# A two-block transformer kernel: the first expert routing in two passes, and the order of the first heads rewritten

## What is computed

```
def peer_ffn(xn, w_pq, sub_keys1, sub_keys2, expert_down, expert_up):   # per block of 128 tokens
    qh = (xb @ w_pq).reshape(T, P_HEADS, 2, P_KEY_DIM)                   # 8 heads, two half queries
    s1, s2 = qh[:, :, 0] @ sub_keys1.T, qh[:, :, 1] @ sub_keys2.T        # 128 scores each
    v1, i1 = top_k(s1, 16); v2, i2 = top_k(s2, 16)
    top_s, pos = top_k(v1[..., :, None] + v2[..., None, :], 16)          # best 16 of the 256 sums
    eidx = (i1 * 128 + i2) at pos
    g = softmax(top_s)
    a = gelu(expert_down[eidx] . xb)
    return sum_k (g * a)_k * expert_up[eidx]_k
```

## Time and profile before

| | us |
|---|---|
| median of three runs | 1513.57 |
| the profiled execution's own time | 1514.97 |
| its span | 1513.2 |
| granted clock, mean over the run | 0.912 |
| busy in the span: PE, DVE, POOL, ACT | 1266.0, 970.1, 510.4, 350.0 |
| moved by DMA | 389.60 MB, of which the gathers' queue 278.15 MB |
| first gather issued | 855.24 |
| last dot product starts | 1504.50 |

### The profile page before, as it was taken

The page is one execution under the profiler, slowest core; times in us unless marked ns, Lnnn a source line. Parts: engine busy times, 40 slices in busy tenths (PEclk is TensorE's granted clock), DMA queues, the critical chain, the costliest instruction groups (busy, mean ns, idle before and its releaser), DMA issues.

```text
span 1513.2 us, 14840 instructions
## 1 busy us (share of the span) xinstructions
PE 1266.0 (84%) x5254; PEld 907.0 (60%) x5254; DVE 970.1 (64%) x1897; ACT 350.0 (23%) x718; POOL 510.4 (34%) x407
## 2 busy tenths in 40 slices
PE   8999999999999999999999998665755666556656
PEld 6776778888888888887888896222222222222222
DVE  7799985153410000324422499999999998999987
ACT  3443433222100000123412332111111211111112
POOL 3367771010000000000010256666545555555550
PEclk9999999999999999999999999888687777887788
DMA  6232333253344444333264499999999999999997
GB/s 265 84 112 84 112 115 137 88 195 139 139 158 148 156 150 151 135 133 112 84 241 180 166 405 414 421 421 421 422 422 422 421 423 422 422 421 422 422 421 298
DMA packets 55018, 389.60 MB, mean 257 GB/s; under 512 B 6192, under 2 KB 6512, under 8 KB 8240
## 3 DMA queue, kind: packets, MB, share of 16 engines
q0 software_dynamic: 38400, 278.15, 44.4%
q1 hardware_dynamic: 16416, 110.64, 20.6%
q10 hardware_dynamic: 144, 0.03, 0.0%
HBM read 387.75 MB, written 1.05 MB: 257 GB/s over the span
## 4 chain that ended last, share of the span: by engine, by line
PE 52%; DVE 21%; DMA 18%; POOL 4%; issue 3%; ACT 2%; DVEq 0%; ACTq 0%; POOLq 0%
PE psD L992 12%; DMA arena<-in_expert,arena 9%; PE psD L935 8%; PE psD L1036 7%; PE psD L416 7%; DMA ring<-in_expert,arena 5%; DMA feat<-in_expert,arena 4%; PE psD L1009 4%; DVE arena L2090 3%; DVE feat L2090 2%; POOL arena L2079 2%; PE psD L1595 2%; DVE ring L2090 2%; PE psD L1366 2%; DVE feat L2123 2%
## 5 line engine op out<-in xcount | busy, mean ns | idle before, releaser
L992 PE MATMUL psD<-feat,ring 128*128 128x256 f32 (+1 forms) x1056 | 234.0, 382 | 5.7 <-DVE feat L370 5.2
L992 PEld LDWEIGHTS psD<-feat,ring 128*128 128x128 f32 x1056 | 201.4, 191 | 34.8 <-issue 6.5
L2079 POOL DMA_INDIRECT feat<-in_expert,arena x77 | 107.9, 1401 | 178.8 <-DVE arena L2050 156.9
L2324 POOL DMA_DIRECT2D feat<-in_xo x3 | 1.7, 554 | 443.4 <-PE psN L345 443.4
L2079 POOL DMA_INDIRECT arena<-in_expert,arena x102 | 132.2, 1296 | 38.1 <-issue 26.8
L2090 DVE CUSTOM_DVE_ANT_0 arena<-arena,feat 128x1024 f32<-128x1024 f32 x102 | 121.5, 1222 | 24.2 <-DMA arena<-in_expert,arena 23.9
L935 PE MATMUL psD<-feat,ring 128*128 128x256 f32 (+1 forms) x576 | 133.5, 390 | 0.0
L1884 PE MATMUL psB<-arena 128*128 128x512 f32 x128 | 82.8, 805 | 50.9 <-ACT arena L1977 50.9
L935 PEld LDWEIGHTS psD<-feat,ring 128*128 128x128 f32 x576 | 108.7, 191 | 24.7 <-issue 8.1
L416 PE MATMUL psD<-feat,ring 128*128 128x256 f32 x512 | 110.8, 379 | 0.0
L1036 PE MATMUL psD<-feat,ring 128*128 128x256 f32 x512 | 110.7, 379 | 0.0
(11 more groups left out here) (559 smaller groups left out, 2201.8 us busy)
## 6 DMA issues: line engine op xcount, KB each, us to landing
ring<-in_w SPq DMA_DIRECT2D x101, 1024.0 KB, 4.8
feat<-in_xo POOLq DMA_DIRECT2D x3, 1024.0 KB, 8.4
feat<-in_pq POOLq DMA_DIRECT2D x2, 1024.0 KB, 11.5
arena<-in_expert,arena POOLq DMA_INDIRECT x102, 22.5
feat<-in_expert,arena POOLq DMA_INDIRECT x77, 19.5
feat<-in_xT SPq DMA_DIRECT2D x2, 544.0 KB, 4.5
arena<-in_w_akv POOLq DMA_DIRECT2D x1, 1024.0 KB, 5.3
feat<-in_memT POOLq DMA_DIRECT2D x1, 1024.0 KB, 5.8
```

Of the source, the lines that this page charges most:

```text
L992: mm = nc.tensor.matmul(psD[:, 2 * (c % 2) + m, 0:T], home[:, k, m * P:(m + 1) * P], x[:, k], start=(k == 0), stop=(k == KT - 1))
L2079: (nc.gpsimd.indirect_dma_start(GPAIR[b], None, a["expert"], bass.IndirectOffsetOnAxis(ap=EID[:, c:c + 1], axis=0)) .then_inc(s_gb[b], 16))
```

## The change

The pieces, by the names above:

- **Routing of group 0 in two passes** (`route_first_dve`, `chosen_dve`). The best 8 keys of each half give 64 sums, whose best 8 are places 0 to 7; their indices are written first. A second pass then finds keys 9 to 16, all 256 sums, blanks the 8 sums that were taken and picks places 8 to 15. `s_eid` rises twice for group 0, so later waits read g + 2.
- **`SOON` has eight buffers in place of nine**, each used twice in group 0. The waits of the first gathers are spread: place 3 waits for `s_xt`, place 4 for `s_xo` (before, place 0 did). The load of the weights `pq5`, 1 MB, which POOL issued ahead of all gathers, stands between places 5 and 6.
- **Block 0's first score is issued in the middle of the second half query.**
- **Head 1's queries come ahead of block 1's head 0 query** on PE: chunk 0 of `pq`, `xturn`, `scores(1)`, then `query0(1, ...)`; block 1's head 0 scores are issued in the middle of the next chunk.
- **ACT's order**: the first Gelu stands before block 1's second state copy; the Gelu of group 0's quarters 2 and 3 stands before the drain of chunks 2 and 3 (it stood before the drain of chunk 3 and before the scores of head 5); Exp of group 1 and its first Gelu are each one head earlier.
- `rstd_dve(1)` on DVE moves behind quarter 1's dots.

```diff
-SOON = [4, 5, 6, 9, 10, 11, 12, 0, 3]
+SOON = [4, 5, 6, 7, 9, 10, 11, 12]
...
-    QBANK = {(0, 0): psB[:, 1], (0, 1): psD[:, 0], (1, 0): psB[:, 0], (1, 1): psB[:, 1]}
-    SBANK = {(0, 0): psD[:, 1], (0, 1): psD[:, 2], (1, 0): psD[:, 2], (1, 1): psD[:, 3]}
+    QBANK = {(0, 0): psB[:, 1], (0, 1): psD[:, 0], (1, 0): psB[:, 0], (1, 1): psD[:, 3]}
+    SBANK = {(0, 0): psD[:, 1], (0, 1): psD[:, 2], (1, 0): psB[:, 0], (1, 1): psY[:, :]}
...
@@ blocks_pe
         query0_pe(0, 0)
-        query0_pe(0, 1)
-        score0_pe(0, 0)
+        query0_pe(0, 1, mid=lambda: score0_pe(0, 0))
         score0_pe(0, 1)
...
         hturn_pe(1, 1)
-        query0_pe(1, 0)
-        query0_pe(1, 1)
-        xturn_pe(1)
-        score0_pe(1, 0)
-        score0_pe(1, 1)
...
@@ blocks_act
         first_gate()
         state_act(1, 0)
+        first_gelu()
         state_act(1, 1)
...
         state_root_act(1)
-        first_gelu()
-        for m in range(2):
-            query0_act(1, m)
-        xturn_act(1)
-        for x in range(2):
-            score0_act(1, x)
+        nc.scalar.activation(F7[:, 1, 3:4], epsc[:, 0:1], ACT.Gelu)
...
@@ peer_pe
+            if h == 1:
+                xturn_pe(1)
+                scores(1)
+                query0_pe(1, 0)
+                query0_pe(1, 1)
...
@@ peer_act
         for h in range(1, PH):
+            if h > 2:
+                scored(h - 1)
+            if h in (3, 4):
+                coefficients(0, h - 1)
+            if h == 5:
+                gate(1)
             if h == 6:
-                coefficients(0, 3)
-            if h > 1:
-                scored(h - 1)
-            if h == 4:
-                coefficients(0, 2)
-            if h == 6:
-                gate(1)
-            if h == 7:
                 gelu(1, 0)
             pair_act(FIRST["pq"], h - 1, QH[:, 2 * h:2 * h + 2])
             if h == 1:
                 coefficients(0, 1)
+                scored(1)
+                xturn_act(1)
+                query0_act(1, 0)
+                query0_act(1, 1)
+                score0_act(1, 0)
+                score0_act(1, 1)
...
+    def route_first_dve(link):
...
+        for x in range(2):
+            v.wait_ge(s_psc, x + 1)
+            link(v.max(VAL[:, x, 0:8], SCO0[:, x]))
+            ins = v.max_index(IDX[:, x, 0:8], VAL[:, x, 0:8], SCO0[:, x])
+        link(ins)
+        v.tensor_copy(IDF8[:, :, :], IDX[:, :, 0:8])
+        link(tt(few.rearrange("p (a b) -> p a b", a=8), VAL[:, 0, 0:8].unsqueeze(2).to_broadcast([P, 8, 8]),
+                VAL[:, 1, 0:8].unsqueeze(1).to_broadcast([P, 8, 8]), ALU.add))
+        link(v.max(TV[:, 0, 0:8], few))
+        link(v.max_index(POS[:, 0, 0:8], TV[:, 0, 0:8], few))
+        v.wait_ge(s_io, 2)
+        chosen_dve(0, 8, 3, link)
+        for x in range(2):
+            ins = v.match_replace(SCO0[:, x], VAL[:, x, 0:8], SCO0[:, x], MAXNEG)
+        link(ins)
+        next8(VAL, IDX, SCO0, 2, link)
...
+        link(v.match_replace(flat_, TV[:, 0, 0:8], flat_, MAXNEG))
+        next8(TV, POS, flat_.unsqueeze(1), 1, link)
+        tt(GT, TV[:, 0], TV[:, 0, 0:1].to_broadcast([P, PTOP]), ALU.subtract)
+        chosen_dve(8, 16, 4, link)
...
@@ gathers_pool
-            nc.gpsimd.wait_ge(s_eid, g + 1)
+            nc.gpsimd.wait_ge(s_eid, g + 2 if g else 1)
             for i in range(PTOP):
                 b = pair(g, i)
+                if g == 0 and i == 8:
+                    nc.gpsimd.wait_ge(s_eid, 2)
                 if b in last:
                     nc.gpsimd.wait_ge(*used(*last[b]))
-                elif b == 3:
-                    nc.gpsimd.wait_ge(s_qh, 4)
+                elif g == 0 and i == 3:
+                    nc.gpsimd.wait_ge(s_xt, 4)
+                elif g == 0 and i == 4:
+                    nc.gpsimd.wait_ge(s_xo, 4)
                 elif g == 0 and i in (6, 7):
+                    if i == 6:
+                        nc.gpsimd.wait_ge(s_xs, 5)
+                        nc.gpsimd.dma_start(PQ5.rearrange("p k n -> p (k n)"), a["pq5"]).then_inc(s_mem, 16)
                     nc.gpsimd.wait_ge(s_h3, 4)
-                elif g == 0 and i == 0:
-                    nc.gpsimd.wait_ge(s_xo, 4)
...
-        for part in range(4):
-            route_dve(0, part, link, first=True)
+        route_first_dve(link)
...
-                if g == q == 0:
+                if g == 0 and q == 1:
                     rstd_dve(1)
...
-        pool.wait_ge(s_xs, 5)
-        pool.dma_start(PQ5.rearrange("p k n -> p (k n)"), a["pq5"]).then_inc(s_mem, 16)
```

More of the change, by code:

```diff
@@ L1110, in build @@
     GT, GN = carve([PTOP]), carve([PTOP])
+    IDF8, PAF8, SEL8 = (carve([2, 8]) for _ in range(3))
+    PA8 = carve([2, 8]).bitcast(U32)
     GM = carve([1])
@@ L1609, in hturn_pe, with query0_pe @@
         mm.then_inc(s_ht, 1)
-    def query0_pe(t, m):
+    def query0_pe(t, m, mid=None):
         if t:
@@ L1752, in score0_act @@
     def score0_act(t, x):
-        nc.scalar.wait_ge(s_ps, 2 * t + x + 1)
+        nc.scalar.wait_ge(s_ps, 3 * t + x + 1)
         if x == 0:
@@ L1780, in blocks_act @@
         state_act(0, 1)
[L1781 to L1784, removed]
+        for m in range(2):
+            query0_act(0, m)
+            score0_act(0, m)
         xturn_act(0)
@@ L1907, in scored @@
         def scored(h):
-            nc.scalar.wait_ge(s_ps, h + 4)
+            nc.scalar.wait_ge(s_ps, h + 4 if h > 1 else 3)
+            if h == 1:
+                nc.scalar.wait_ge(s_rs, 2)
             for t in range(2):
@@ L1944, in gate @@
     def gate(g):
-        nc.scalar.wait_ge(s_eid, g + 1)
+        nc.scalar.wait_ge(s_eid, g + 2)
         nc.scalar.activation(GT, GT, ACT.Exp, accum_out=GM)
@@ L1951, in first_gate @@
         gate(0)
-        nc.scalar.activation(F7[:, 1, 3:4], epsc[:, 0:1], ACT.Sqrt)
     def gelu(g, q):
@@ L2018, in route_dve @@
+    def route_dve(g, part, link, t=0):
+        tt = nc.vector.tensor_tensor
+        src = SCOH
         sums = CS.rearrange("p a b -> p (a b)").unsqueeze(1)
@@ L2020, in route_dve @@
         if part == 0:
-            for r in ((0, 1), (1, 2)) if first else ((0, 2),):
-                r = slice(*r)
-                if t == 0:
-                    nc.vector.wait_ge(s_psc, r.stop if first else g + 4)
-                if not first:
-                    link(nc.vector.tensor_scalar(SCOH, SCO.rearrange("p t x n -> p (t x) n")[:, bass.ds(2 * g, 2)], 1.0,
-                                                 None, ALU.mult))
-                top8(VAL[:, r], IDX[:, r], src[:, r], r.stop - r.start, link)
-                next8(VAL[:, r], IDX[:, r], src[:, r], r.stop - r.start, link)
+            if t == 0:
+                nc.vector.wait_ge(s_psc, 3 if isinstance(g, int) and g == 1 else g + 4)
+            link(nc.vector.tensor_scalar(SCOH, SCO.rearrange("p t x n -> p (t x) n")[:, bass.ds(2 * g, 2)], 1.0,
+                                         None, ALU.mult))
+            top8(VAL, IDX, src, 2, link)
+            next8(VAL, IDX, src, 2, link)
         if part == 1:
```

54 lines of the change are left out of this document (40 added, 14 removed).

## The result

The changed kernel takes 1518.57 us (median of 11 runs, 1517.05 to 1520.43). The kernel before takes 1514.88 (11 runs). The ratio is 1.0027, with a 95% interval of 1.0018 to 1.0035: slower by 2.7 to 5.3 us. The forecast was 1514.6, +1.0 us, with 1517.0 as the upper end of its range. It stood on three runs of the kernel before (1513.57); with all eleven the same +1.0 would have read 1515.9, so 1.3 us of the 4.0 between forecast and time are the base, and the rest is the change. The profiled execution has a span of 1516.6 us against 1513.2, so its trace shows 3.4 of the 4 us.

What follows compares the result with a forecast made beforehand. DMA bytes at 421 GB/s bound the expert part: earlier start and closed hole -5.3, new hole before place 13 +5.2, restart +1.1, sum +1.0 on 1513.57, so 1514.6 us; its own range 1512.4 to 1516.5, overall 1511.3 to 1517.0.

Steps and rivals of the forecast that it cites:

- What bounds the kernel: Expert part: megabytes at 421 GB/s set the time; only an earlier first gather, a closed hole or a tail shortens it.
- The first indices: Group 0's routing: the first pass ends at 849.7, so the first gather goes at 849.95, 5.3 us earlier.
- the new stream: Gathers from place 0 on: place 7 lands at 876.4; unhindered, group 1's place 13 lands at 933.7, a gain of 5.3 us.
- What is late next: ACT: quarter 3's Gelu ahead of chunk 3's drain makes PE 6.0 us late at head 4's scores, at 910.4.
- Nothing gives that back: chunks 4 to 6 follow each other without a gap: PE after head 4's scores: the 6.0 us lateness carries to the last chunk, so group 1's place 13 goes at 932.9.
- the dry stretch at 930: Stream before group 1's place 13: a new hole of +5.2 us and its restart of +1.1 us.
- in time for a turn to land at 898.7: Group 1's indices were to come at 892.2, early enough to leave no hole in the stream.
- the hole at 905: Stream before group 1's place 2: closing this hole was to give 2.6 of the 5.3 us gain.
- The quarter 2 Gelu ... stalls PE by under 1 us, inside the 6.0: ACT ahead of chunk 2's drain: a PE stall under 1 us, adding nothing to the 6.0 us lateness.
- The first Gelu: ACT before block 1's second state copy: costs nothing, as place 3's dot comes at 865.2 against 865.96 for the copy.
- ACT's order does not bite: Faster rival: the stream keeps its whole 5.3 us, less a little at other waits; 1508.5 us, chance 0.12.
- Descriptors are slow beside a busy DVE: Slower rival: POOL's issues cost 0.9 us more at first gather and restart; +3.4, 1517.0 us, chance 0.13.

Runs made afterwards that it cites:

- e1: Changed kernel with ACT's order alone undone for the Gelus of quarters 2 and 3 and group 1's Exp and first Gelu; 1511.44 us, ratio 0.9979 to before.
- e3: Changed kernel with eleven useless matmuls on PE before head 4's scores, filling its wait; 1516.65 us, ratio 1.0008 to the kernel before.
- e7: e1 with the Gelu of quarter 2 again ahead of chunk 2's drain, as in the changed kernel; 1514.02 us, ratio 0.9995 to the kernel before.
- e8: e1 with the first Gelu back behind block 1's turned state, as in the kernel before; 1515.85 us, ratio 1.0010 to the kernel before.
- e2: e1 with POOL's first gather held back until the second routing pass; 1518.19 us, ratio 1.0024 to the kernel before.
- e5: e1 with the last weight chunk loaded one chunk earlier, into another ring slot; 1511.50 us, ratio 0.9978 to the kernel before.
- e4: Kernel before with only ACT's new order in the loop over heads; 1522.12 us, ratio 1.0049 to the kernel before.

## Why the prediction was wrong

**What bounds the kernel** held: bytes at 421 GB/s, holes and the start. The byte account agrees with the times to 0.1 us for four of the nine rows above, which is closer than one execution can promise, and to 0.5 for two more.

**The first indices, the new stream up to place 7** held: 850.02 for 849.95, and place 7's dot at 876.83 for a landing at 876.4.

**What is late next** named the right wait. Quarter 3's last dot at 908.51 (908.2), PE at head 4's scores at 910.61 (910.4), released by ACT, 6.2 us late (6.0). e1 shows it as the cause of the whole loss.

**The step that failed** is the sentence "Nothing gives that back: chunks 4 to 6 follow each other without a gap", and with it "It goes at 926.92 + 6.0 = 932.9". The chunks do follow without a gap, but I took their lengths from a PE that had not waited. Behind a wait of 4.73 us the clock is 0.50 and the same matmuls take 3.1 us more; place 13 goes at 936.22. e3 takes the fall of the clock away and leaves the wait: 5.78 us in place of 7.90, and 2.9 us off the time. With 3.1 added, my +1.0 is +4.1, the measured value (2.7 to 5.3); that it meets it to a tenth is luck, for the sizes below were off too. The Trainium skill says it in the page "TensorE: Matmul & The Clock Gate" (The HAM clock gate): the throttled state is the default, and activity releases it. The trace agrees, 0.50 in the stretch behind the wait, then 0.83 and 1.00 while PE stays busy; I had looked at what the wait delays, and not at what it does to the work behind it. The trace of the kernel before could have told me. Near its start PE waits 5.17 us and then runs 64 matmuls of one group; these are that row and the two stretches from 15 us on:
```profile
15.18 16.87 PE L992 MATMUL psD<-feat,ring 128*128 128x272 f32 x64 [5.17 <-DVE feat L370]
```
```profile
15.00:20.00 5.00, 4.82 (x13) 3.76 (x14) 4.89 (x20) 0.00 (x0) 0.00 (x0) 0.58 1.03 415
20.00:25.00 5.00, 5.00 (x23) 4.16 (x22) 4.86 (x17) 0.18 (x1) 3.95 (x2) 1.00 0.91 376
```
In the first 5 us it gets through 13 matmuls at a clock of 0.58, in the next through 23 at 1.00.

**Two sizes beside it** were off, and nearly cancel, since bytes that are lost earlier make the dry stretch at 930 shorter. Group 1's indices were to be "in time for a turn to land at 898.7". They came when I said (892.65 for 892.2), but the queue was nearly empty by then, and the restart lost what I had charged at two other restarts and not here: 1.2 us by bytes, 1.4 in e1. And the dry stretch at 930 was to cost 5.2 + 1.1 = 6.3 us; it cost 7.6. Of the hole at 905 the trace gave 2.0 us back, not 2.6. So the stream came to 930 with 1.2 + 0.6 us less in hand, and place 13 was 3.3 us later than I had it: 6.3 + 3.3 - 1.8 = 7.8 against 7.6.

**"The quarter 2 Gelu ... stalls PE by under 1 us, inside the 6.0"** fits this trace (0.81) and not e7, where the wait is 1.90 us and the version loses 2.4 us. I treated it as a fixed number, and it moves with the landings of group 0.

**The first Gelu** was costed at nothing and is worth 4.7 us (e8) in this kernel. It was right that its move hurts no one here. But the forecast put the whole stream 5 us earlier and did not say that this needs the Gelu at 865, because the ninth gather waits for a buffer that is read behind it. e2 (early Gelu, late rows) and e8 (early rows, late Gelu) are both slower than the kernel before.

**The rivals.** *ACT's order does not bite* fell: it bites for 7.3 us. *Descriptors are slow beside a busy DVE* also fell: the first issue took 1.04 us beside the second pass against 1.03 before, and place 7 was on time. The time came out near that rival's (1517.0) for another reason. The chance of 0.13 for slower was small because every rival I priced was a shift of times and none changed how long the work takes.

What stays open is the division of the 7.3 us between the Gelus of quarters 2 and 3, and where the last 0.5 us of e5 goes.

## What to carry to other kernels

When an edit makes an engine wait in the middle of dense work, price the wait and the work behind it: look in the trace that you have for what equal matmuls take behind a wait, wherever in the program it stands, and use that duration. An instruction that is moved ahead in one queue is paid for by everything behind it there, so ask of each moved wait when its releaser comes, not when it used to come. And before a hole in the stream is closed, find what opens the next one: in e5 closing 1.4 us of it opened 0.9.

## What the runs showed of the hardware

Behind a wait of PE the matmuls took 3.1 us more in the changed kernel (wait of 4.73 us, clock 0.50 in the next 5 us), 1.8 and 1.8 in e4 (4.14 and 3.07 us, 0.70 and 0.66), 1.7 in e2 (5.55 us), 1.7 in e8 (3.13 us) and 1.8 in e7 (1.90 us, 0.66). Behind 0.81 us in the changed kernel and 0.98 us in e3 the rest of the chunk took the full-speed 5.78 us. In these eight cases the price does not follow the length of the wait, and that 1.90 us were enough once was not expected.

Matmuls of no use in a wait were worth their place in e3, where the clock held: 11 products (22 in the trace), 4.91 us, took 2.9 us, give or take 2, off the program.

A stream that is only nearly dry when the next group's gathers are issued loses bytes as well: 1.2 us in the changed kernel and 1.4 in e1 at 895, with the DMA share still at 0.98 in the changed kernel's stretch. The share alone does not show such a hole; the GB/s do (333).
